# A two-layer hybrid backbone on one core: the down products of the expert passes one step further behind

## The chip, the cores and the metric

The kernel runs on one core of a Trainium2 chip. The metric is the device time in microseconds (us) of one execution, as the median of several runs; lower is better.

## The reference

The model has two layers over 512 tokens of width 1024 (256 of context, 256 latent). Each layer mixes tokens (a gated long convolution, a pooling mixer and an eight-head latent attention, joined by one output projection) and then mixes channels: a dense SwiGLU in layer 0, and in layer 1 a top-2-of-8 expert SwiGLU on the 256 latent tokens only. The change is in the experts:

```python
def swiglu(h, wg, wu, wd):
    return (jax.nn.silu(h @ wg) * (h @ wu)) @ wd

def moe_swiglu(h, w_router, wg, wu, wd):
    logits = (h @ w_router).astype(F32)
    top_val, top_idx = lax.top_k(logits, TOP_K)
    gates = jax.nn.softmax(top_val, axis=-1)
    comb = jnp.sum(jax.nn.one_hot(top_idx, N_EXPERTS, dtype=F32) * gates[..., None], axis=-2)
    out = jnp.zeros(h.shape, F32)
    for e in range(N_EXPERTS):
        out = out + comb[..., e:e + 1] * swiglu(h, wg[e], wu[e], wd[e]).astype(F32)
    return out.astype(h.dtype)
```

Here h is 256 x 1024, wg and wu are 1024 x 2816 and wd is 2816 x 1024 for each of 8 experts, all in fp32.

## The kernel before

**Passes.** The experts' part is eight passes, `expert_pass(i)` for i = 0 to 7, one for each expert. (Two further pairs of passes stand behind a branch on the number of tokens of an expert; they are not taken with these inputs.) For each expert up to 128 tokens are gathered by a matmul with a selection matrix (`gather`, for two experts at a time), and the result of pass i is spread back to the 256 token rows in pass i + 1 (`spread` on TensorE, `add_up` on VectorE, both at steps 2 and 4).

**Steps and granules.** The 2816 hidden columns are done in FC = 11 steps s of 256. A step has three granules of weights, each 128 x 2048 fp32 (1 MB): two for gate and up, `("gu", s, 0)` and `("gu", s, 1)`, each half of the 1024 input rows, and one for down, `("d", s, 0)`. NGR = 33 granules make a pass; `lay` writes them into memory in the order in which the program uses them, and `fpos` gives a granule's place in this order.

**Three products for one.** fp32 accuracy comes from pairs of rounded numbers: every operand has a high half (the number rounded to fp32r by a cast) and a low half (the rest), and `split3` (lines 446 to 450) issues high x high, high x low and low x high. A granule takes 4 of these triples, 12 matmuls of 512 columns.

**What each engine does in a step.** TensorE: `gate_up(s, 0)` and `gate_up(s, 1)` sum gate and up of the step into PSUM bank s % 2; `turn_h` (line 1003) transposes the gated rows in two 128 x 128 transposes into bank 2; `down` (line 1012) multiplies these with the down granule and sums over all steps into banks 4 and 5. ScalarE: `high(i, j)` (line 1505) makes the high half of granule j; Silu of the gate (line 1530); `high_turned` (line 1514), the high half of the transposed rows. VectorE: `low(i, j)` (line 2272) makes the low half of a granule; the product of Silu and up, `hh` (line 2298); `low_turned` (line 2281), the low half of the transposed rows. In pass 0, VectorE also runs `plan_passes`, a series of small operations on the routing tables, at the end of steps 1 to 7, and ScalarE `diagonal`, eight activations of 128 x 128, at the end of step 0. In the last pass GpSimd adds the residual (`add_residual`, lines 2471 and 2473).

**The two rings.** SP loads granules into six raw buffers: granule n goes into its buffer when VectorE has made the low half of granule n - 6 (`expert_stream`, line 2390). The high and low halves have three slots: `high(i, j)` waits until TensorE has used granule j - 3 (the counter `x_used`), `low(i, j)` waits for `high(i, j)`, and TensorE waits for `low(i, j)`.

**What sets the order.** Nothing is scheduled by a planner. Each engine's program is written out by hand in `expert_pass`, once for each engine, and each engine takes its instructions in this order; the three orders and the order of the granules in memory have to agree. TensorE's order of a step is `gu(s,0)`, transposes of step s - 1, `gu(s,1)`, `down(s-1)`; in the last step the transposes of step 10 stand in the middle of `down(9)`. At the start of a pass the place in the ring also holds the previous pass's last granules; ScalarE and VectorE there save the previous output (`save_y`, `split_y`, lines 1498 and 2230).

Of the kernel before, what the change touches and what calls it, by code (L numbers as in the profile page):

```python
# [13 lines left out]
F32 = mybir.dt.float32  # L14
# [3 lines left out]
ALU = mybir.AluOpType  # L18
ACT = mybir.ActivationFunctionType
# [26 lines left out]
RING = 3  # L46
# [21 lines left out]
def ffn_order():  # L68

    order = []  # L70
    for s in range(FC):
        order += [("gu", s, 0), ("gu", s, 1)]
        if s:
            order.append(("d", s - 1, 0))
    return order + [("d", FC - 1, 0)]


# [59 lines left out]
def build(nc, io, table):  # L137
    with ExitStack() as ctx:
# [211 lines left out]
        def x_slot(j):  # L350

            return (j + XOFF) % RING

        def tokens_of(i):

            own = slice(P * (i % 2), P * (i % 2) + P)
            if (i // 2) % 2:
                return odd_hi[:, :, own], odd_lo[:, :, own]
            own = slice(256 + P * (i % 2), 384 + P * (i % 2))
            return hT_hi[:, :, own], hT_lo[:, :, own]  # L360
# [23 lines left out]
        order = ffn_order()  # L384
        fpos = {x: i for i, x in enumerate(order)}

# [38 lines left out]
        def _(eng):  # L425
# [543 lines left out]
            def expert_pass(i):  # L969
# [41 lines left out]

                def down(s, fs=(0, 1)):
                    j = fpos[("d", s, 0)]
                    hi, lo = granule_of(j)
                    eng.wait_ge(x_tlo, FC * i + s + 1)
                    if s == 0 and i:
                        eng.wait_ge(x_y, 2 * i)
                    for f in fs:
                        a = slice(P * f, P * f + P)
                        for n in range(2):  # L1020
                            cs = slice(1024 * f + 512 * n, 1024 * f + 512 * n + 512)
                            last = split3(PS[:, 4 + n, :], f_hi[:, s % 2, a], f_lo[:, s % 2, a], hi[:, cs], lo[:, cs],
                                          s == 0 and f == 0, s == FC - 1 and f == 1)
                    if fs[-1]:
                        last.then_inc(x_used, 1)

                m = i // 2
                for s in range(FC):
                    if s == 0:
                        eng.wait_ge(x_glo, 4 * m + 2)  # L1030
                    gate_up(s, 0)
                    if s:
                        turn_h(s - 1)
                    if s == 0:
                        eng.wait_ge(x_glo, 4 * m + 4)
                    gate_up(s, 1)
                    if s == FC - 1:
                        down(s - 1, (0,))
                        turn_h(s)
                        down(s - 1, (1,))  # L1040
                    elif s:
                        down(s - 1)
                    if i and i not in LAST and s in (2, 4):
# [5 lines left out]
                    if i == 0 and s == 2:  # L1049
                        gates()  # L1050
                down(FC - 1)

# [58 lines left out]
        def _(eng):  # L1111
# [395 lines left out]
            def expert_pass(i):  # L1507
# [8 lines left out]
                if i:  # L1516
                    for j in range(0 if i in LAST else 1, RING):
                        high(i, j)
                    if i not in LAST:
                        save_y(i)  # L1520
                for s in range(FC):
                    if s:
                        high_turned(s - 1)
                    if s + 1 < FC:
                        for j in range(fpos[("gu", s + 1, 0)] if s else RING, fpos[("gu", s + 1, 1)] + 1):
                            high(i, j)
                    else:
                        high(i, fpos[("d", s, 0)])
                    eng.wait_ge(x_used, NGR * i + fpos[("gu", s, 1)] + 1)
                    act(sg[:, s % 2, :], PS[:, s % 2, 0:256], ACT.Silu).then_inc(x_silu, 1)  # L1530
                    if s + 1 < FC:
                        high(i, fpos[("d", s, 0)])
                    else:
                        high_turned(s)
                        if i + 1 not in LAST:
                            high(i + 1, 0)
# [80 lines left out]
        def _(eng):  # L1617
# [650 lines left out]

            def low(i, j, halves=(0, 1)):
                eng.wait_ge(x_hi, NGR * i + j + 1)  # L2270
                q = slice(1024 * halves[0], 1024 * halves[-1] + 1024)
                last = v.tensor_tensor(w_lo[:, x_slot(j), q], x_raw(NGR * (i % 2) + j)[:, q],  # L2272
                                       w_hi[:, x_slot(j), q].bitcast(F32), ALU.subtract)
                if halves[-1]:
                    last.then_inc(x_lo, 1)

            def expert_pass(i):
# [11 lines left out]
                for s in range(FC):  # L2289
                    if s:  # L2290
                        low_turned(s - 1)
                    if s + 1 < FC:
                        for j in range(fpos[("gu", s + 1, 0)] if s else RING, fpos[("gu", s + 1, 1)] + 1):
                            low(i, j)
                    else:
                        low(i, fpos[("d", s, 0)], (0,))
                    eng.wait_ge(x_silu, FC * i + s + 1)
                    v.tensor_tensor(hh[:, s % 2, :], PS[:, s % 2, 256:512], sg[:, s % 2, :],
                                    ALU.mult).then_inc(x_h, 1)
                    low(i, fpos[("d", s, 0)], (0, 1) if s + 1 < FC else (1,))  # L2300
                    if i and i not in LAST and s in (2, 4):
# [183 lines left out]
def lay(inputs):  # L2485
# [17 lines left out]
    def swiglu(wg, wu, wd):  # L2503
# [4 lines left out]
        d5 = wd.reshape(n, FC, 2, P, D)  # L2508
        for i, (kind, s, half) in enumerate(ffn_order()):
            if kind == "gu":  # L2510
# [108 lines left out]
```

## Time and profile before

| What | Value |
|---|---|
| Median of 3 runs | 1689.28 us |
| The runs | 1684.3, 1690.0, 1689.28 us |
| Span of the profiled execution | 1686.8 us |
| TensorE busy (matmuls) | 1611.4 us, 96% |
| TensorE weight loads busy | 1269.6 us, 75% |
| VectorE busy | 1289.9 us, 76% |
| ScalarE busy | 897.8 us, 53% |
| Mean granted TensorE clock | 0.982 |
| Bytes read from HBM | 401.03 MB, 238 GB/s over the span |

The span runs from the first to the last instruction of one profiled execution; for this execution no other time was taken, so its span stands for it, and the median of the runs is 2.5 us above the span. Shares of busy time are averages over the whole program. The expert passes take the last 800 us of it, and in them all shares are higher than in the table. Matmuls are pipelined: a matmul of 512 columns is recorded with a duration of about 0.39 us, though the next starts 0.23 us after it, so durations of matmuls overlap and the distance of their starts is the better measure. In waits, the engine named behind the arrow is the one whose signal came last.

### The profile page before, as it was taken

Reading aid. Unit: us, or ns where it says so; the run is one execution under the profiler, and the core shown is the slowest. Engines: PE = TensorE matmul, PEld = TensorE weight load, DVE = VectorE, ACT = ScalarE, POOL = GpSimd, SP = SyncE. Lnnn points to the kernel's source line nnn. Section 1 sums busy time; section 2 is a strip of 40 time slices with the busy share of each in tenths; the row PEclk is TensorE's granted clock in tenths of the full one; section 3 lists DMA queues with packets and bytes.
Section 4 is the critical chain, followed back from the end, with each engine's and each line's share of the span. In section 5 each row is a group of like instructions: output and inputs, shape, how many; then the busy total and the mean of one; then the engine's idle time right before and its main releaser. Section 6 shows DMA issues by size and latency. Waiting matters only on the chain.

```text
span 1686.8 us, 19520 instructions
## 1 busy us (share of the span) xinstructions
PE 1611.4 (96%) x7452; PEld 1269.6 (75%) x7452; DVE 1289.9 (76%) x1723; ACT 897.8 (53%) x1029; POOL 40.7 (2%) x40
## 2 busy tenths in 40 slices
PE   5999999899999999999899999999999999999996
PEld 2785567778888888786587778888888888888875
DVE  3944473698777865765768998898988889898997
ACT  3324363332222222444657777767777776777764
POOL 1000000000000000000000000000000000000050
PEclk8999999899999999999989999999999999999999
DMA  9225511363455544232147999899989999899982
GB/s 392 86 75 196 222 54 45 131 228 130 170 193 207 203 171 150 74 122 94 43 175 302 361 361 337 348 359 353 359 349 357 346 359 352 342 350 374 366 318 114
DMA packets 55972, 403.43 MB, mean 239 GB/s; under 512 B 6417, under 2 KB 6449, under 8 KB 8769
## 3 DMA queue, kind: packets, MB, share of 16 engines
q1 hardware_dynamic: 53712, 387.47, 60.3%
q0 software_dynamic: 2160, 14.63, 2.3%
q8 instruction: 62, 1.02, 0.2%
q14 instruction: 38, 0.30, 0.1%
HBM read 401.03 MB, written 1.05 MB: 238 GB/s over the span
## 4 chain that ended last, share of the span: by engine, by line
PE 74%; DVE 16%; ACT 5%; issue 3%; DMA 2%; SPq 0%; DVEq 0%; ACTq 0%
PE PS L448 20%; PE PS L450 20%; PE PS L449 20%; DVE w_lo L2272 6%; PE PS L753 2%; DVE w_lo L1633 2%; DMA arena<-in_ada 2%; ACT w_hi L1505 1%; DVE arena L1646 1%; PE PS L1008 1%; DVE XT L1999 1%; PE PS L765 1%; PE PS L778 1%; PE PS L732 1%; PE PS L458 1%
## 5 line engine op out<-in xcount | busy, mean ns | idle before, releaser
L2272 DVE TENSOR_TENSOR w_lo<-arena,w_hi 128x2048 fp32r<-128x2048 f32 (+1 forms) x136 | 305.9, 2254 | 43.3 <-ACT w_hi L1505 43.3
L2272 DVE TENSOR_TENSOR w_lo<-raw,w_hi 128x2048 fp32r<-128x2048 f32 (+1 forms) x133 | 298.9, 2251 | 32.9 <-ACT w_hi L1505 32.4
L1505 ACT CAST w_hi<-arena 128x2048 fp32r<-128x2048 f32 x132 | 251.5, 1909 | 46.2 <-PE PS L450 46.2
L1505 ACT CAST w_hi<-raw 128x2048 fp32r<-128x2048 f32 x129 | 246.9, 1916 | 43.5 <-PE PS L450 43.5
L448 PE MATMUL PS<-hT_hi,w_hi 128*128 128x512 f32 (+1 forms) x576 | 216.1, 375 | 8.6 <-DVE hT_lo L1779 6.9
L449 PE MATMUL PS<-hT_lo,w_hi 128*128 128x512 f32 (+1 forms) x576 | 213.7, 371 | 0.0
L450 PE MATMUL PS<-hT_hi,w_lo 128*128 128x512 f32 (+1 forms) x576 | 213.5, 371 | 0.0
L448 PE MATMUL PS<-w_hi,hT_hi 128*128 128x512 f32 (+1 forms) x448 | 178.5, 398 | 0.9 <-DVE w_lo L1633 0.6
L450 PE MATMUL PS<-w_hi,hT_lo 128*128 128x512 f32 (+1 forms) x448 | 174.6, 390 | 0.0
L449 PE MATMUL PS<-w_lo,hT_hi 128*128 128x512 f32 (+1 forms) x448 | 173.5, 387 | 0.0
L448 PE MATMUL PS<-w_hi,f_hi 128*128 128x512 f32 x352 | 140.4, 399 | 2.1 <-DVE f_lo L2281 2.1
L1633 DVE TENSOR_TENSOR w_lo<-raw,w_hi 128x2048 fp32r<-128x2048 f32 (+1 forms) x54 | 122.3, 2265 | 24.1 <-ACT w_hi L1127 23.9
L449 PE MATMUL PS<-w_lo,f_hi 128*128 128x512 f32 x352 | 139.0, 395 | 0.0
L450 PE MATMUL PS<-w_hi,f_lo 128*128 128x512 f32 x352 | 138.7, 394 | 0.0
L448 PE MATMUL PS<-w_hi,odd_hi 128*128 128x512 f32 x336 | 135.5, 403 | 0.0
L1127 ACT CAST w_hi<-raw 128x2048 fp32r<-128x2048 f32 (+1 forms) x54 | 102.2, 1892 | 60.8 <-PE PS L450 52.1
L448 PEld LDWEIGHTS PS<-hT_hi,w_hi 128*128 128x128 f32 x576 | 109.4, 190 | 30.1 <-DVE hT_lo L1779 7.6
L450 PE MATMUL PS<-w_hi,odd_lo 128*128 128x512 f32 x336 | 131.8, 392 | 0.0
L449 PE MATMUL PS<-w_lo,odd_hi 128*128 128x512 f32 x336 | 131.0, 390 | 0.0
L450 PEld LDWEIGHTS PS<-hT_hi,w_lo 128*128 128x128 f32 x576 | 109.5, 190 | 18.7
L449 PEld LDWEIGHTS PS<-hT_lo,w_hi 128*128 128x128 f32 x576 | 109.6, 190 | 18.3
L1999 DVE SCALAR_TENSOR_TENSOR XT<-PS,mod,XT 128x256 f32<-128x256 f32 x200 | 84.7, 476 | 33.6 <-PE PS L450 33.2
(322 smaller groups left out, 2536.0 us busy)
## 6 DMA issues: line engine op xcount, KB each, us to landing
raw<-in_moe SPq DMA_DIRECT2D x132, 1024.0 KB, 5.2
arena<-in_moe SPq DMA_DIRECT2D x132, 1024.0 KB, 5.2
raw<-in_ffn SPq DMA_DIRECT2D x33, 1024.0 KB, 4.8
raw<-in_dot SPq DMA_DIRECT2D x28, 1024.0 KB, 4.8
raw<-in_ada SPq DMA_DIRECT2D x17, 1024.0 KB, 6.5
raw<-in_out SPq DMA_DIRECT2D x8, 1024.0 KB, 4.9
raw<-in_inb SPq DMA_DIRECT2D x8, 960.0 KB, 4.7
raw<-in_ina SPq DMA_DIRECT2D x5, 1024.0 KB, 5.2
```

Of the source, the lines that this page charges most:

```text
L448: mm(out, s_hi, m_hi, start=start, stop=False)
L449: mm(out, s_hi, m_lo, start=False, stop=False)
L450: return mm(out, s_lo, m_hi, start=False, stop=stop)
L458: i = mm(o[32 * k:32 * k + 32, :], cpad[:, 4 * half + k, :], w[:, 512 * k:512 * k + 512], start=half == 0, stop=half == 1)
L732: i = mm(o[:, 256 * j:256 * j + 256], wuq[:, k, h, :], cqT[:, k, 256 * s:256 * s + 256], start=k == 0, stop=k == KQ - 1)
L753: i = mm(o[:, q], qT[0:96, n // 2, a:a + P], KT[0:96, h, 0:512 if s else 256], start=True, stop=True)
L765: i = nc.tensor.transpose(o[:, to:to + P], prob[:, u % 4, at:at + P], ident[:, :])
L1127: nc.scalar.copy(w_hi[:, slot[n], 0:w], raw_at(n)[:, 0:w]).then_inc(act_done, 1)
L1505: nc.scalar.copy(w_hi[:, x_slot(j), :], x_raw(n)).then_inc(x_hi, 1)
L1633: v.tensor_tensor(w_lo[:, slot[n], 0:w], raw_at(n)[:, 0:w], w_hi[:, slot[n], 0:w].bitcast(F32), ALU.subtract).then_inc(dve_done, 1)
L1999: v.scalar_tensor_tensor(out=XT[:, k, q], in0=o[:, q], scalar=mod[:, l, j + k, s:s + 1], in1=XT[:, k, q], op0=ALU.mult, op1=ALU.add).then_ ...
L2272: last = v.tensor_tensor(w_lo[:, x_slot(j), q], x_raw(NGR * (i % 2) + j)[:, q], w_hi[:, x_slot(j), q].bitcast(F32), ALU.subtract)
```

## The change

The granules of an expert pass are used, and stored in memory, in another order: in step s TensorE does both gate-up halves of step s, then the transposes of the gated rows of step s - 1, then the down product of step s - 2. The first two steps of a pass have no down product, and three stand after the eleventh step's gate-up halves, with the last transposes between the first and the second of them. The new function `pass_order` gives this order, and `next_granules` gives for each step the granule that ScalarE and VectorE prepare before the Silu and the gated rows of the step (`ahead`) and those that they prepare after the turned rows of the step before (`behind`). The turned rows of step s - 1 are now split after the Silu and the gated product of step s, not ahead of them. The cut of a low half into two pieces in the last step goes. The dense feed forward of layer 0 keeps its order (`ffn_order`). No instruction of TensorE, ScalarE or GpSimd is added or removed; VectorE has one instruction fewer in each pass.

```diff
@@ -73,6 +73,16 @@
         if s:
             order.append(("d", s - 1, 0))
     return order + [("d", FC - 1, 0)]
+
+
+def pass_order():
+
+    order = []
+    for s in range(FC):
+        order += [("gu", s, 0), ("gu", s, 1)]
+        if s > 1:
+            order.append(("d", s - 2, 0))
+    return order + [("d", FC - 2, 0), ("d", FC - 1, 0)]
 
 
 def filter_beside(b):
@@ -351,6 +361,14 @@
 
             return (j + XOFF) % RING
 
+        def next_granules(s):
+
+            if s == 0:
+                return [RING], []
+            if s == FC - 1:
+                return [fpos[("d", s - 1, 0)]], [fpos[("d", s, 0)]]
+            return [fpos[("gu", s + 1, 0)]], [fpos[("gu", s + 1, 1)], fpos[("d", s - 1, 0)]]
+
         def tokens_of(i):
 
             own = slice(P * (i % 2), P * (i % 2) + P)
@@ -382,7 +400,7 @@
             return raw[:, place[g], :] if place[g] < RING else first_raw[place[g] - RING]
 
         order = ffn_order()
-        fpos = {x: i for i, x in enumerate(order)}
+        fpos = {x: i for i, x in enumerate(pass_order())}
 
         def width(kind):
             return 4 * HB if kind == "inb" else GRAN
@@ -1009,37 +1027,32 @@
                                                    ident[:, :])
                     last.then_inc(x_turned, 1)
 
-                def down(s, fs=(0, 1)):
+                def down(s):
                     j = fpos[("d", s, 0)]
                     hi, lo = granule_of(j)
                     eng.wait_ge(x_tlo, FC * i + s + 1)
                     if s == 0 and i:
                         eng.wait_ge(x_y, 2 * i)
-                    for f in fs:
+                    for f in range(2):
                         a = slice(P * f, P * f + P)
                         for n in range(2):
                             cs = slice(1024 * f + 512 * n, 1024 * f + 512 * n + 512)
                             last = split3(PS[:, 4 + n, :], f_hi[:, s % 2, a], f_lo[:, s % 2, a], hi[:, cs], lo[:, cs],
                                           s == 0 and f == 0, s == FC - 1 and f == 1)
-                    if fs[-1]:
-                        last.then_inc(x_used, 1)
+                    last.then_inc(x_used, 1)
 
                 m = i // 2
                 for s in range(FC):
                     if s == 0:
                         eng.wait_ge(x_glo, 4 * m + 2)
                     gate_up(s, 0)
-                    if s:
-                        turn_h(s - 1)
                     if s == 0:
                         eng.wait_ge(x_glo, 4 * m + 4)
                     gate_up(s, 1)
-                    if s == FC - 1:
-                        down(s - 1, (0,))
-                        turn_h(s)
-                        down(s - 1, (1,))
-                    elif s:
-                        down(s - 1)
+                    if s:
+                        turn_h(s - 1)
+                    if s > 1:
+                        down(s - 2)
                     if i and i not in LAST and s in (2, 4):
                         spread(i, s // 4)
                     if i % 2 and i + 1 < NE and s in (3, 5, 7, 9):
@@ -1048,6 +1061,8 @@
                         turn_pick(m)
                     if i == 0 and s == 2:
                         gates()
+                turn_h(FC - 1)
+                down(FC - 2)
                 down(FC - 1)
 
             def last_spread(i):
@@ -1519,18 +1534,16 @@
                     if i not in LAST:
                         save_y(i)
                 for s in range(FC):
+                    ahead, behind = next_granules(s)
+                    for j in ahead:
+                        high(i, j)
+                    eng.wait_ge(x_used, NGR * i + fpos[("gu", s, 1)] + 1)
+                    act(sg[:, s % 2, :], PS[:, s % 2, 0:256], ACT.Silu).then_inc(x_silu, 1)
                     if s:
                         high_turned(s - 1)
-                    if s + 1 < FC:
-                        for j in range(fpos[("gu", s + 1, 0)] if s else RING, fpos[("gu", s + 1, 1)] + 1):
-                            high(i, j)
-                    else:
-                        high(i, fpos[("d", s, 0)])
-                    eng.wait_ge(x_used, NGR * i + fpos[("gu", s, 1)] + 1)
-                    act(sg[:, s % 2, :], PS[:, s % 2, 0:256], ACT.Silu).then_inc(x_silu, 1)
-                    if s + 1 < FC:
-                        high(i, fpos[("d", s, 0)])
-                    else:
+                    for j in behind:
+                        high(i, j)
+                    if s == FC - 1:
                         high_turned(s)
                         if i + 1 not in LAST:
                             high(i + 1, 0)
@@ -2266,13 +2279,10 @@
                                                   op0=ALU.mult, op1=ALU.add)
                 last.then_inc(x_late, 1)
 
-            def low(i, j, halves=(0, 1)):
+            def low(i, j):
                 eng.wait_ge(x_hi, NGR * i + j + 1)
-                q = slice(1024 * halves[0], 1024 * halves[-1] + 1024)
-                last = v.tensor_tensor(w_lo[:, x_slot(j), q], x_raw(NGR * (i % 2) + j)[:, q],
-                                       w_hi[:, x_slot(j), q].bitcast(F32), ALU.subtract)
-                if halves[-1]:
-                    last.then_inc(x_lo, 1)
+                v.tensor_tensor(w_lo[:, x_slot(j), :], x_raw(NGR * (i % 2) + j), w_hi[:, x_slot(j), :].bitcast(F32),
+                                ALU.subtract).then_inc(x_lo, 1)
 
             def expert_pass(i):
 
@@ -2287,17 +2297,16 @@
                     if i not in LAST:
                         split_y(i)
                 for s in range(FC):
-                    if s:
-                        low_turned(s - 1)
-                    if s + 1 < FC:
-                        for j in range(fpos[("gu", s + 1, 0)] if s else RING, fpos[("gu", s + 1, 1)] + 1):
-                            low(i, j)
-                    else:
-                        low(i, fpos[("d", s, 0)], (0,))
+                    ahead, behind = next_granules(s)
+                    for j in ahead:
+                        low(i, j)
                     eng.wait_ge(x_silu, FC * i + s + 1)
                     v.tensor_tensor(hh[:, s % 2, :], PS[:, s % 2, 256:512], sg[:, s % 2, :],
                                     ALU.mult).then_inc(x_h, 1)
-                    low(i, fpos[("d", s, 0)], (0, 1) if s + 1 < FC else (1,))
+                    if s:
+                        low_turned(s - 1)
+                    for j in behind:
+                        low(i, j)
                     if i and i not in LAST and s in (2, 4):
                         (add_up if i < NE else add_late)(i, s // 4)
                     if i % 2 and i + 1 < NE:
@@ -2506,7 +2515,7 @@
         gu = out.reshape(n, 3 * FC, P, 4, 2, 256)
         g6, u6 = (w.reshape(n, 2, 4, P, FC, 256) for w in (wg, wu))
         d5 = wd.reshape(n, FC, 2, P, D)
-        for i, (kind, s, half) in enumerate(ffn_order()):
+        for i, (kind, s, half) in enumerate(pass_order()):
             if kind == "gu":
                 gu[:, i, :, :, 0, :] = g6[:, half, :, :, s, :].transpose(0, 2, 1, 3)
                 gu[:, i, :, :, 1, :] = u6[:, half, :, :, s, :].transpose(0, 2, 1, 3)
```

How the instructions move, at the start of a pass. ScalarE first, at the start of pass 4, from the casts of the saved output on. `w_hi` is the high half of a granule, the `x_full` semaphore in its wait counts up with the raw buffers and so tells the granules apart (full3 is granule 3 of this pass, full4 is 4, full5 is 5, full0 is 6, full1 is 7); `ACTIVATE` is the Silu, `f_hi` the high half of the turned rows. Before:

```order
L1498 CAST y_hi<-PS 128x512
L1505 CAST w_hi<-arena 128x2048 [waits x_full3,x_used]
L1530 ACTIVATE arena<-PS 128x256 [waits x_used]
L1505 CAST w_hi<-arena 128x2048 [waits x_full4,x_used]
L1514 CAST f_hi<-PS 128x256 [waits x_used,x_turned]
L1505 CAST w_hi<-arena 128x2048 [waits x_full5,x_used]
L1505 CAST w_hi<-raw 128x2048 [waits x_full0,x_used]
L1530 ACTIVATE arena<-PS 128x256 [waits x_used]
L1505 CAST w_hi<-raw 128x2048 [waits x_full1,x_used]
```

And after, at the same place of ScalarE's program:

```order
L1513 CAST y_hi<-PS 128x512
L1520 CAST w_hi<-arena 128x2048 [waits x_full3,x_used]
L1541 ACTIVATE arena<-PS 128x256 [waits x_used]
L1520 CAST w_hi<-arena 128x2048 [waits x_full4,x_used]
L1541 ACTIVATE arena<-PS 128x256 [waits x_used]
L1529 CAST f_hi<-PS 128x256 [waits x_used,x_turned]
L1520 CAST w_hi<-arena 128x2048 [waits x_full5,x_used]
L1520 CAST w_hi<-raw 128x2048 [waits x_full0,x_used]
L1520 CAST w_hi<-raw 128x2048 [waits x_full1,x_used]
```

The cast of granule 5 stood behind the turned rows of step 0 and ahead of the second Silu; now it stands behind both. Granule 5 was the first half of step 2's gate-up, and is now the second half of it (granule 4, which was the first down granule, is now the first half).

TensorE at the start of pass 2, where it waits for a new granule or for a product of another engine. The rows left out are the other eleven matmuls of a granule. `w_hi,odd_hi` is the first matmul of a gate-up half, `w_hi,f_hi` that of a down product, and `ident,arena` the transposes. Before, from the second gate-up half of step 0 on:

```order
L448 MATMUL PS<-w_hi,odd_hi 128x512 [waits x_lo,x_gathered_lo]
...
L448 MATMUL PS<-w_hi,odd_hi 128x512 [waits x_h,x_lo]
...
L1008 MATMUL PS<-ident,arena 128x128 [waits x_turned_lo,x_h]
...
L448 MATMUL PS<-w_hi,odd_hi 128x512 [waits x_lo]
...
L448 MATMUL PS<-w_hi,f_hi 128x512 [waits x_y_split,x_turned_lo,x_lo]
```

And after, from the same matmul to the first down product:

```order
L466 MATMUL PS<-w_hi,odd_hi 128x512 [waits x_lo,x_gathered_lo]
...
L466 MATMUL PS<-w_hi,odd_hi 128x512 [waits x_h,x_lo]
...
L466 MATMUL PS<-w_hi,odd_hi 128x512 [waits x_lo]
...
L1026 MATMUL PS<-ident,arena 128x128 [waits x_turned_lo,x_h]
...
L466 MATMUL PS<-w_hi,odd_hi 128x512 [waits x_h,x_lo]
...
L466 MATMUL PS<-w_hi,odd_hi 128x512 [waits x_lo]
...
L1026 MATMUL PS<-ident,arena 128x128 [waits x_turned_lo,x_h]
...
L466 MATMUL PS<-w_hi,f_hi 128x512 [waits x_y_split,x_turned_lo,x_lo]
```

The transposes of step 0 stand behind the second half of step 1, and the first down product stands behind six gate-up halves where it stood behind four.

## Rows read from the trace of the kernel before

**Rows 1.** Busy time by stretch (us busy, count), one pass; last: clock, DMA share, GB/s
```profile
990.00:1086.00 96.00, 95.88 (x442) 77.98 (x441) 85.62 (x68) 68.91 (x60) 0.00 (x0) 1.00 0.90 345
```

**Rows 2.** Waits, 900 to 1650 us: who on whom, us total, times, longest
```profile
ACT f_hi L1514 <- PE PS L1008: 112.0, 83, 2.9
...
PEld PS L1008 <- DVE arena L2298: 7.0, 10, 1.1
```

**Rows 3.** Timeline of TensorE, one step: start, us, what
```profile
1109.09 0.38 PE L1008 MATMUL PS<-ident,arena 128*128 128x128 f32 x2
...
1109.23 0.48 PE L448 MATMUL PS<-w_hi,odd_hi 128*128 128x512 f32 x1
...
1109.54 0.39 PE L449 MATMUL PS<-w_lo,odd_hi 128*128 128x512 f32 x1
...
1112.07 0.39 PE L448 MATMUL PS<-w_hi,f_hi 128*128 128x512 f32 x1
...
1114.86 0.39 PE L448 MATMUL PS<-w_hi,odd_hi 128*128 128x512 f32 x1
...
1117.58 0.38 PE L1008 MATMUL PS<-ident,arena 128*128 128x128 f32 x2
```

**Rows 4.** Timeline of ScalarE, the same step (bracket: idle before, releaser)
```profile
1109.51 0.37 ACT L1514 CAST f_hi<-PS 128x256 fp32r<-128x256 f32 x1 [1.96 <-PE PS L1008]
1109.78 1.91 ACT L1505 CAST w_hi<-arena 128x2048 fp32r<-128x2048 f32 x1
...
1115.06 1.92 ACT L1505 CAST w_hi<-raw 128x2048 fp32r<-128x2048 f32 x1 [0.60 <-PE PS L450]
```

**Rows 5.** Timeline of VectorE, the same step
```profile
1111.72 2.29 DVE L2272 TENSOR_TENSOR w_lo<-arena,w_hi 128x2048 fp32r<-128x2048 f32 x1 [0.20 <-ACT w_hi L1505]
```

**Rows 6.** Timeline of VectorE at the start of pass 2, and one row of ScalarE
```profile
1080.60 6.70 DVE L2272 TENSOR_TENSOR w_lo<-raw,w_hi 128x2048 fp32r<-128x2048 f32 x3 [1.37 <-ACT w_hi L1505]
...
1082.59 1.92 ACT L1505 CAST w_hi<-raw 128x2048 fp32r<-128x2048 f32 x1 [0.22 <-PE PS L450]
...
1087.21 1.28 DVE L2230 TENSOR_TENSOR y_lo<-PS,y_hi 128x512 fp32r<-128x512 f32 x2
1088.41 2.28 DVE L2272 TENSOR_TENSOR w_lo<-arena,w_hi 128x2048 fp32r<-128x2048 f32 x1
1090.61 0.41 DVE L2298 TENSOR_TENSOR arena<-PS,arena 128x256 f32<-128x256 f32 x1
```

**Rows 7.** Timeline of TensorE, the same place
```profile
1090.55 0.39 PE L450 MATMUL PS<-w_hi,odd_lo 128*128 128x512 f32 x1
1091.08 0.44 PE L1008 MATMUL PS<-ident,arena 128*128 128x128 f32 x2
```

**Rows 8.** Timeline of pass 0: three waits of TensorE, one row of VectorE
```profile
897.67 0.50 PE L448 MATMUL PS<-w_hi,hT_hi 128*128 128x512 f32 x1 [0.29 <-DVE w_lo L2272]
...
904.52 0.47 PE L448 MATMUL PS<-w_hi,f_hi 128*128 128x512 f32 x1 [0.81 <-DVE f_lo L2281]
...
923.30 0.42 DVE L2281 TENSOR_TENSOR f_lo<-PS,f_hi 128x256 fp32r<-128x256 f32 x1
...
923.87 0.47 PE L448 MATMUL PS<-w_hi,f_hi 128*128 128x512 f32 x1 [0.30 <-DVE f_lo L2281]
```

**Rows 9.** Timeline of TensorE, last pass, while GpSimd works
```profile
1625.65 0.44 PE L1008 MATMUL PS<-ident,arena 128*128 128x128 f32 x2 [0.62 <-DVE arena L2298]
```

**Rows 10.** Timeline of TensorE after its longest idle stretches; a window by stretch
```profile
41.74 0.77 PE L448 MATMUL PS<-hT_hi,w_hi 128*128 128x512 f32 x1 [3.29 <-DVE hT_lo L1779]
...
45.20 0.39 PE L450 MATMUL PS<-hT_hi,w_lo 128*128 128x512 f32 x1
...
40.00:45.00 5.00, 3.26 (x8) 2.61 (x9) 5.00 (x14) 3.07 (x8) 0.00 (x0) 0.50 0.98 402
...
1673.41 0.50 PE L965 MATMUL PS<-y_hi,pickT 128*128 128x512 f32 x1 [2.00 <-DVE y_lo L2230]
```

**Rows 11.** DMA issues of expert weights, 990 to 1600 us
```profile
DMA to landing us min/median/max: 4.6/5.3/7.9
```

## The prediction

> **What bounds the kernel now.** I read the table of busy time by stretch first. The expert passes are eight stretches of 96 to 100 us, from about 887 us to 1671 us of the span; [rows 1] gives one window of 96 us in them: TensorE is busy 95.88 us of it at a granted clock of 1.00, VectorE 85.62, ScalarE 68.91. The reader is to see that TensorE is full, and that VectorE has only some 10 us left in 96. Busy time alone could mislead, since matmuls overlap, so the next view is the table of waits over the passes [rows 2]: ScalarE stood 112 us before the cast of the turned rows, which no one missed, and TensorE's weight loads stood 7.0 us before the transposes, for the gated rows of VectorE. That is nearly all that TensorE waits for here. The timeline of one step [rows 3] gives the prices. The pair of transposes starts at 1109.09, the next pair at 1117.58: a step of 8.49 us, for 36 matmuls and one pair. Twelve matmuls and the pair take 1112.07 - 1109.09 = 2.98, the twelve of the down product 1114.86 - 1112.07 = 2.79. Nothing stands idle between them. So in the middle of a pass the time is the number of matmuls, and the change leaves this number as it is; it can act only through TensorE's few waits and through waits that it makes.
>
> **The supply of granules.** Each granule of weights passes three slots. ScalarE casts it (high half) as soon as the granule three places earlier has been used, VectorE then makes the low half, and only then may TensorE start it. From [rows 4] and [rows 5]: the product that frees a slot ends in the row where the next one starts, 1114.86, and the cast starts at 1115.06, 0.20 later. A small cast or Silu (128x256) holds ScalarE 0.27 (1109.51 to 1109.78). The cast starts at 1109.78 and its low half at 1111.72, 1.94 later, and takes 2.29. A waiting matmul starts 0.15 after VectorE's end (923.30 + 0.42 = 923.72, matmul at 923.87) [rows 8], and the one behind it another 0.08 late (0.31 apart in place of 0.23). I count in these.
>
> **Part 1: the middle of a pass (s = 2 to 9).** I call the four pieces G0(s) and G1(s) (gate-up halves), T (transposes) and D (down). Before: G0(s) T(s-1) G1(s) D(s-1). After: G0(s) G1(s) T(s-1) D(s-2). The cast of G1(s+1) now stands behind Silu(s) and the cast of the turned rows, both of which need the end of G1(s). Counted from that end: Silu at 0.20, turned rows at 0.47 (the transposes' result is there at 0.42, 1109.09 to 1109.51), cast of G1(s+1) at 0.74, low half from 2.68 to 4.97. TensorE meanwhile does T, D and G0, 2.98 + 2.79 = 5.77. Margin 0.65 after the 0.15. The other two granules have over 1 us. T(s-1) and D(s-2) now use what was ready a step ago. Cost 0, and the cover is that 0.65; VectorE's work in a step stays 3 x 2.29 + 2 x 0.4, 7.7 of 8.49.
>
> **Part 2: the start of each pass, the term that decides.** At s = 1 there is no D yet (D(0) comes at s = 2), so six gate-up halves follow each other: G0(0) G1(0) G0(1) G1(1) T(0) G0(2) G1(2) T(1) D(0). ScalarE's order is written by the same rule as in the middle: cast of G0(2), Silu(1), turned rows (0), cast of G1(2), cast of D(0). The slot of G1(2) was freed by G0(1), long before; but its cast is behind Silu(1), which waits for the end of G1(1). From there the supply chain needs 0.20 + 0.27 + 0.27 + 1.94 + 2.29 + 0.15 = 5.12, and TensorE has only T(0) and G0(2) to do, 2.98. It stands 2.14, and with the 0.08 behind it loses 2.2. In before, the corresponding wait does not exist, since D(0) was the fifth granule. ScalarE takes its instructions in the order of the program: in [rows 2] it stood 112 us for transposes while the cast behind had its slot free. The wait comes in all eight passes: 8 x 2.2 = 17.6 us. In pass 0 the eight small activations of `diagonal` stand ahead of the cast of G0(2), so part of the wait may fall one piece earlier, at G0(2); the later cast, of G1(2), still has to follow Silu(1), which starts when G1(1) ends, so I keep the same sum. Behind the stall everything has time: D(0)'s low half ends 7.2 after the end of G1(1), needed at 8.1; the SP queue and the transfers see their slots freed later by the stall alone, and at worst 7.9 us to landing [rows 11] stand against the two steps between casts of one buffer, 16.98, less the 1.94 and 2.29 until it is released: 12.7. Bounds for this term: 0 if something covers it, 8 x 2.7 = 21.6 if VectorE's low half should start only after other work of 0.5.
>
> **Part 3: waits that go.** (a) At the start of passes 1 to 7 VectorE is a chain: three low halves in 6.70, two of the saved output in 1.28, one more low half, and then the gated rows at 1090.61 [rows 6], for which T(0) waits: it starts 0.53 after the matmul before it in place of 0.23 [rows 7]. T(0) now stands behind G1(1). What is late next is that G1(1) itself: its low half was done at 1090.69, TensorE would start it at 1090.78. The chain starts earlier after the change, since the cast of the next pass's first granule no longer waits for the late T(10): the cast that waits longest, for the end of D, starts at 1082.59 [rows 6]; from there 1.94, one low half 2.2, the output's 1.28 and the last low half 2.2 end at about 1090.2. So all 0.3 is kept: 7 x 0.3 = 2.1. (b) In pass 0 VectorE also plans the later passes, in many small operations, ahead of the low half of the turned rows, and D waits (the first of the five waits is for a granule): idle 0.29, 0.81 and three times about 0.30, of which the first stands in [rows 8]; each costs its idle time, plus 0.39 - 0.23 = 0.16 and 0.08. Sum 2.0 + 5 x 0.24 = 3.2. After the change that low half stands ahead of the planning, with a step to spare. The planning now uses up the margin of the granules: VectorE has 8.49 - 7.7 = 0.8 free in a step and the planning wants more than that, so the margin shrinks in each step. I take 3.0, bounds 0.5 and 3.2. (c) In the last pass GpSimd's residual slows VectorE's low halves, and TensorE waits for VectorE in three steps, 0.62 in the one shown [rows 9]. VectorE's work is the same after, it is the bound there, and the loss stays: 0, bounds -1 and +1.
>
> **Sum.** 17.6 - 2.1 - 3.0 = +12.5 us on the profiled execution's 1686.8 us of span: 1699.3. The runs shown have a median of 1689.3 (1684.3 to 1690.0), 2.5 above that span, which I carry along: 1701.8.
>
> **Rivals.**
> B, not slower: TensorE catches up. For it: TensorE's weight loads are busy 78 of 96 us [rows 1]; with 18 us of room a pass, a late start of 2.2 us would be made good, and only part 3 would be left: 1689.3 - 5.1 = 1684.2. It decides as soon as the matmuls behind a wait can run closer than 0.23 apart. Against: in [rows 3] they stand 0.23 apart with no wait, in any step. The Trainium skill (Perfetto Trace Analysis, Identifying the Most-Contended Engine) says to judge TensorE's headroom by its weight loads and not by matmul busy time; by it B would be likelier than I hold it, but the spacing of the starts is the stronger evidence here.
> C, the margin of 0.65 in the middle isn't there: if the low half of G1 comes 0.25 late in each of eight steps of eight passes, 16 us are added: 1718. For it: VectorE is the fullest after TensorE, 85.62 of 96 [rows 1]. Against: every count above closes with idle time left.
> D, the clock: after an idle stretch TensorE comes back at half clock. In [rows 10] it stood 3.29 us, the window around shows a granted clock of 0.50 (1.2 GHz), and the eight matmuls from 41.74 to 45.20 took 3.46 against 8 x 0.23 = 1.84: 1.6 us a time, 8 x 1.6 = 12.8: 1714.6. Against: before the last spread it stood 2.00 us, about what I expect of the new wait, and the matmul behind is 0.50, not 0.77. The Trainium skill (TensorE: Matmul & The Clock Gate, Part 1: The HAM clock gate) holds that idleness throttles the engine to half rate; that the trace agrees where it stood 3.29 and does not where it stood 2.00 is why D gets little.
>
> **How the numbers follow.** Forecast 0.76, B 0.12, C 0.07, D 0.05. The forecast's own range is 1697 to 1707: parts 2 and 3 at 2.0 to 2.5 a pass and with pass 0's saving lost at the upper end, and about 2 for the spread of the median. B and C are left out, so the range over all is 1692 to 1716. A change of 0.5%, 8.4 us, is about what a measurement can tell here from none. Slower by more: nearly all of the forecast, C and D, less a little because +12.5 is not far above 8.4: 0.80. Same: most of B and the low end of the forecast, 0.15. Faster: 0.05; all the waits that could go, 5.1 us and the last pass's, don't sum to much over 8.4.
>
> **What would show it.** In the trace after: in each pass one matmul of a gate-up half, about 6 us before the first down product begins, that waits for the low half of w with 1.7 to 2.3 us of idle time, eight times in all; seen from VectorE, an idle stretch before that low half for ScalarE's cast, and from ScalarE a wait for the matmuls ahead of Silu(1). Each pass some 1.9 longer (2.2 less 0.3). No wait for the gated rows at the transposes before the last pass, and none for the turned rows at D in pass 0. Steps of 8.49 as before in the middle. Wrong would be: no such wait (then B or a cover that I don't see), or the same wait repeated in each step (C), or matmuls 0.43 apart behind it (D).

## Result and profile after

The changed kernel takes 1705.31 us (median of 4 runs, 1700.0 to 1707.28), the kernel before 1686.79 (4 runs beside them, 1683.91 to 1690.0). The ratio is 1.0094, with a 95% interval of 1.0077 to 1.0111: slower by about 16 us. The two medians are 18.5 apart, the spans of the two profiled executions 16.7, and the 0.0094 of the ratio are 15.9; what follows explains the 16.7 of the spans. The prediction was 1701.8 us, +12.5. The profiled execution took 1705.29 us, its span is 1703.5 us (before 1686.8), and the mean granted clock fell from 0.982 to 0.974.

The window by stretch that answers to [rows 1]; the columns are the same:

```profile
990.00:1086.00 96.00, 94.10 (x430) 77.10 (x429) 83.55 (x64) 66.14 (x56) 0.00 (x0) 0.98 0.90 334
```

TensorE, full before, misses 1.9 us here, and the granted clock is not 1.00 any more. The waits over the passes, 900 to 1665 us, that answer to [rows 2] (total, times, longest):

```profile
ACT w_hi L1520 <- PE PS L468: 117.8, 139, 2.6
ACT arena L1541 <- PE PS L468: 103.0, 84, 3.4
DVE w_lo L2284 <- ACT w_hi L1520: 74.5, 183, 1.3
PEld PS L466 <- DVE w_lo L2284: 20.2, 14, 2.3
PE PS L466 <- DVE w_lo L2284: 14.5, 11, 1.9
...
ACT f_hi L1529 <- PE PS L1026: 5.4, 7, 0.8
```

The weight loads' 7.0 us for the gated rows are gone from the answer, and of ScalarE's 112 us before the cast of the turned rows 5.4 are left; it now stands before the Silu instead (L1541). New is TensorE's wait for low halves of granules: 14.5 us in 11 pieces. Seven of these are the same wait, in passes 1 to 7. At the start of pass 2, the timeline of TensorE:

```profile
1095.34 0.38 PE L1026 MATMUL PS<-ident,arena 128*128 128x128 f32 x2
...
1098.08 0.39 PE L468 MATMUL PS<-w_hi,odd_lo 128*128 128x512 f32 x1
1100.37 0.50 PE L466 MATMUL PS<-w_hi,odd_hi 128*128 128x512 f32 x1 [1.90 <-DVE w_lo L2284]
1100.70 0.52 PE L467 MATMUL PS<-w_lo,odd_hi 128*128 128x512 f32 x1
1101.02 0.63 PE L468 MATMUL PS<-w_hi,odd_lo 128*128 128x512 f32 x1
1101.44 0.63 PE L466 MATMUL PS<-w_hi,odd_hi 128*128 128x512 f32 x1
1101.87 0.63 PE L467 MATMUL PS<-w_lo,odd_hi 128*128 128x512 f32 x1
```

and of ScalarE and VectorE at the same place:

```profile
1095.53 0.38 ACT L1541 ACTIVATE arena<-PS 128x256 f32<-128x256 f32 x1 [3.27 <-PE PS L468]
1095.81 0.37 ACT L1529 CAST f_hi<-PS 128x256 fp32r<-128x256 f32 x1
1096.07 1.92 ACT L1520 CAST w_hi<-arena 128x2048 fp32r<-128x2048 f32 x1
...
1098.02 2.29 DVE L2284 TENSOR_TENSOR w_lo<-arena,w_hi 128x2048 fp32r<-128x2048 f32 x1 [1.31 <-ACT w_hi L1520]
```

The first matmul of the second gate-up half of step 2 waits: 2.29 between starts where 0.23 is the rule. ScalarE had stood 3.27 us before the Silu, with the cast behind it. From the transposes (the end of G1(1)) to the matmul it is 1100.37 - 1095.34 = 5.03; the prediction had counted 5.12. So far this is part 2. But two rows on, at 1101.02, the matmuls are 0.43 apart and last 0.63: half clock. It starts 0.65 us after the wait has ended and lasts seven matmuls. The windows say so directly; the first is around this wait, the second around the same wait in pass 4:

```profile
1096.00:1104.00 8.00, 6.10 (x20) 4.50 (x19) 6.69 (x5) 5.58 (x4) 0.00 (x0) 0.80 0.68 256
1299.00:1307.00 8.00, 6.10 (x28) 4.69 (x27) 7.16 (x5) 6.16 (x6) 0.00 (x0) 1.00 0.70 270
```

Both have 6.10 us of busy TensorE in 8; the first at a mean clock of 0.80 with 20 matmuls, the second at 1.00 with 28. Six of the seven waits (passes 1, 2, 3, 5, 6, 7) are followed by such a stretch, six or seven matmuls 0.43 apart; the one in pass 4 is not.

Where the time went, from the first matmul of each pass to that of the next (for pass 7 to the start of its last down matmul):

| Pass | Before | After | Difference |
|---|---|---|---|
| 0 | 99.36 | 97.54 | -1.82 |
| 1 | 99.98 | 102.67 | +2.69 |
| 2 | 96.44 | 99.16 | +2.72 |
| 3 | 99.93 | 102.67 | +2.74 |
| 4 (clock stays up) | 96.44 | 97.60 | +1.16 |
| 5 | 99.97 | 102.70 | +2.73 |
| 6 | 96.45 | 99.20 | +2.75 |
| 7 | 99.39 | 101.16 | +1.77 |
| sum | 787.96 | 802.70 | +14.74 |

Of the span's 16.7 us, 1.2 lie ahead of pass 0 and 0.7 behind the last down product, where the program is the same. Pass 4 against the others separates the two costs: the clock takes 2.73 - 1.16 = 1.57 us a time. The rest, +1.16, is the wait (2.29 - 0.23 + 0.08 = 2.14) less 0.30 for the transposes that no longer wait (0.24 behind the matmul before them at 1095.34; 0.53 in [rows 7]) and less about 0.7 that the prediction did not have. Most of that 0.7 is in the steps. The transposes of two neighbouring steps, which answer to the first and last row of [rows 3]:

```profile
1132.06 0.38 PE L1026 MATMUL PS<-ident,arena 128*128 128x128 f32 x2
1132.19 0.47 PE L466 MATMUL PS<-w_hi,f_hi 128*128 128x512 f32 x1
...
1135.06 0.39 PE L466 MATMUL PS<-w_hi,odd_hi 128*128 128x512 f32 x1
...
1140.50 0.38 PE L1026 MATMUL PS<-ident,arena 128*128 128x128 f32 x2
```

A step is 8.44 where it was 8.49, some 0.5 over a pass. The rows show where in the step: before, the gate-up half behind the transposes took 2.84 (1109.23 to 1112.07 in [rows 3]) and the other one 2.72 (1114.86 to 1117.58); now both stand clear of the transposes and take 5.44 together (1135.06 to 1140.50), 0.12 less. The down product, which now stands behind the transposes, takes 2.87 (1132.19 to 1135.06) where it took 2.79 (1112.07 to 1114.86), 0.08 more. Why the gate-up half loses more behind the transposes than the down product does is not shown, nor where the last 0.2 of the 0.7 is.

In pass 0 the turned rows are no longer waited for (the two later waits that [rows 8] shows, and two more like them); the new wait stands there too, in two pieces. This is the first, for granule 4:

```profile
896.77 0.50 PE L466 MATMUL PS<-w_hi,hT_hi 128*128 128x512 f32 x1 [1.24 <-DVE w_lo L2284]
```

and the second, for granule 5, has 0.37 us of idle time. All five waits of before are gone here, 3.2 us by the prediction's count; the two new ones cost 2.1 and the shorter steps give 0.7, which makes the table's -1.8. The clock stays up behind the 1.24 us. In the last pass, during GpSimd's residual, three waits of 0.24 to 0.29 us for granules take the place of those that [rows 9] shows one of:

```profile
1648.35 0.50 PE L466 MATMUL PS<-w_hi,odd_hi 128*128 128x512 f32 x1 [0.29 <-DVE w_lo L2284]
```

### The profile page after: what moved, and what is told of

It is laid out like the page before. It is cut to its first block, busy times and chain, and to the rows that moved or that the text cites. A ratio compares the mean times of both kernels' runs of the same rounds, so it can differ in the third digit from the quotient of the medians.

```text
span 1703.5 us, 19504 instructions
## 1 busy us (share of the span) xinstructions
PE 1617.1 (95%) x7452; PEld 1280.1 (75%) x7452; DVE 1289.3 (76%) x1715; ACT 896.1 (53%) x1029; POOL 42.8 (3%) x40
## 4 chain that ended last, share of the span: by engine, by line
PE 80%; DVE 11%; ACT 4%; issue 3%; DMA 2%; SPq 0%; DVEq 0%; ACTq 0%
PE PS L466 22%; PE PS L468 21%; PE PS L467 21%; DVE w_lo L2284 2%; PE PS L771 2%; DVE w_lo L1646 2%; DMA arena<-in_ada 2%; DVE arena L1659 1%; PE PS L796 1%; PE PS L783 1%; DVE XT L2012 1%; PE PS L750 1%; ACT w_hi L1520 1%; PE PS L1026 1%; PE PS L476 1%
## 5 line engine op out<-in xcount | busy, mean ns | idle before, releaser
L2284 DVE TENSOR_TENSOR w_lo<-arena,w_hi 128x2048 fp32r<-128x2048 f32 x132 | 305.6, 2317 | 46.5 <-ACT w_hi L1520 45.8
L2284 DVE TENSOR_TENSOR w_lo<-raw,w_hi 128x2048 fp32r<-128x2048 f32 x129 | 297.9, 2312 | 34.8 <-ACT w_hi L1520 34.2
L466 PE MATMUL PS<-w_hi,f_hi 128*128 128x512 f32 x352 | 146.0, 415 | 0.1
L1646 DVE TENSOR_TENSOR w_lo<-raw,w_hi 128x2048 fp32r<-128x2048 f32 (+1 forms) x54 | 122.4, 2266 | 23.9 <-ACT w_hi L1142 23.7
```

The lines of the kernel that those rows point to most:

```text
L466: mm(out, s_hi, m_hi, start=start, stop=False)
L1646: v.tensor_tensor(w_lo[:, slot[n], 0:w], raw_at(n)[:, 0:w], w_hi[:, slot[n], 0:w].bitcast(F32), ALU.subtract).then_inc(dve_done, 1)
L2284: v.tensor_tensor(w_lo[:, x_slot(j), :], x_raw(NGR * (i % 2) + j), w_hi[:, x_slot(j), :].bitcast(F32), ALU.subtract).then_inc(x_lo, 1)
```

## Experiments

**Theory.** The letters here are those of the expectations, not of the prediction's rivals. (A) The waits of passes 1 to 7 come from the place of one cast in ScalarE's program, and the half clock comes from these waits. **Rivals:** (B) six gate-up halves in a row drain the three slots whatever ScalarE's order is; (C) the half clock has another cause than the wait.

**1. The cast of granule 5 ahead of the second Silu.**

```diff
         def next_granules(s):
...
+            if s == 1:
+                return [fpos[("gu", 2, 0)], fpos[("gu", 2, 1)]], [fpos[("d", 0, 0)]]
             if s == FC - 1:
```

> The changed kernel with one thing different: in step 1 the cast and the low half of granule 5 (the second gate-up half of step 2) stand ahead of the second Silu. Theory A (the new wait of 1.90 us at the start of passes 1 to 7 comes from this cast standing behind Silu(1), and TensorE's half clock behind it comes from the wait): the wait and the stretches of matmuls 0.43 us apart both go. From the changed kernel's 1705.3 that takes 7 x 2.14 = 15.0 for the waits, 6 x 1.57 = 9.4 for the clock and about 1.9 in pass 0: about 1679, 0.5% under the kernel before. Rival B (the wait comes from the granule supply as such, six gate-up halves in a row drain the ring, whatever the order of ScalarE): the wait moves to another granule and most stays, about 1700. Rival C (the half clock is independent of the wait): the waits go and the clock stays, about 1688.

Measured: 1680.3 us (5 runs, 1678.41 to 1683.19), ratio to before 0.9949, interval 0.9935 to 0.9962. No matmul waits in passes 1 to 6, none is slow. Its window for [rows 1], and the place of the wait:

```profile
990.00:1086.00 96.00, 96.00 (x447) 79.16 (x446) 86.69 (x68) 69.95 (x60) 0.00 (x0) 1.00 0.94 352
```

```profile
1088.87 0.38 PE L1028 MATMUL PS<-ident,arena 128*128 128x128 f32 x2
...
1091.63 0.39 PE L470 MATMUL PS<-w_hi,odd_lo 128*128 128x512 f32 x1
1091.85 0.39 PE L468 MATMUL PS<-w_hi,odd_hi 128*128 128x512 f32 x1
```

The same two matmuls are 0.22 apart. B and C fall; about 25 us hang on the place of one cast and its low half. The passes 1 to 6 are 98.9 and 95.4 us, 1.07 shorter than before: 0.30 for the transposes and 0.77 as in the section above. This version beats both kernels.

It also answers a question by its end. All kernels have the 2.00 us wait ahead of the last spread ([rows 10], last row). Here it reads:

```profile
1661.69 0.65 PE L985 MATMUL PS<-y_hi,pickT 128*128 128x512 f32 x1 [2.00 <-DVE y_lo L2245]
1662.13 0.63 PE L986 MATMUL PS<-y_lo,pickT 128*128 128x512 f32 x1
1662.56 0.63 PE L985 MATMUL PS<-y_hi,pickT 128*128 128x512 f32 x1
```

The same wait, and half clock behind it, which the kernel before did not show. The length of a wait alone does not decide. The other kernels bear this out: behind this wait the eight matmuls run at full clock in the kernel before, in the changed kernel and in experiments 4 and 6, and in experiments 2, 3 and 5 the last two or three of them are 0.38 to 0.43 us apart.

**2 and 3. The wait filled, wholly and by half.** The granule is as late as in the changed kernel, but TensorE does matmuls that nobody reads meanwhile (8, or 4 with `range(4)`).

```diff
                 def gate_up(s, half):
                     j = fpos[("gu", s, half)]
+                    if s == 2 and half == 1 and 0 < i < NE:
...
+                        for _ in range(8):
+                            mm(PS[:, 7, :], pickT[:, (i - 1) % 2, 0:P], y_hi[:, 0:512], start=True, stop=True)
                     if j:
                         hi, lo = granule_of(j)
```

> The changed kernel with eight extra matmuls of 512 columns (their result is overwritten and read by nobody) ahead of the wait for granule 5 in passes 1 to 7; eight take 1.84 us of the 1.90 us of idle time, so that TensorE waits no longer than before by the clock on the wall but does not stand idle. Theory A (idleness costs the clock): no matmuls 0.43 apart at the pass starts, the 9.4 us of the clock go, the 15 us of the waits stay: about 1696. Rival C (the clock falls for another reason, for example the run of six gate-up halves without a down product): no change, 1705.

> As the kernel with eight, but with four extra matmuls: 0.92 us filled, about 1.0 us of idle time left. If the clock falls by the length of the idle time, fewer of the seven passes show half clock than the six of the changed kernel: I expect 0 to 2, 1696 to 1699. If any idle time does it, six again and 1705. Rival C: 1705.

Measured: 1694.96 us with eight (6 runs; ratio 1.0036, 1.0024 to 1.0048) and 1695.13 with four (6 runs; 1.0038, 1.0025 to 1.0052). With four, at the same place of pass 2:

```profile
1091.83 1.09 PE L1003 MATMUL PS<-y_hi,pickT 128*128 128x512 f32 x4
1093.87 0.50 PE L466 MATMUL PS<-w_hi,odd_hi 128*128 128x512 f32 x1 [0.95 <-DVE w_lo L2291]
1094.21 0.40 PE L467 MATMUL PS<-w_lo,odd_hi 128*128 128x512 f32 x1
```

No stretch at half clock behind the wait in any pass of either; passes 1 to 6 take 101.1 and 97.6 us, as pass 4 of the changed kernel does. So idleness costs the clock, 10 us in all, and half of the idle time filled is enough here: the seven waits that are left with four matmuls have 0.95 or 0.96 us of idle time. More matmuls made the kernel 10 us faster. It stays slower than before: the waits remain.

**4. The kernel before, planning behind the turned rows.** Part 3b by itself.

```diff
                     if s:
                         low_turned(s - 1)
+                        if i == 0:
+                            plan_passes(s - 1)
...
-                    if i == 0:
-                        plan_passes(s)
```

> The kernel before with one thing different: in pass 0 VectorE's planning operations of a step stand behind the low half of the turned rows instead of ahead of it. My part 3b says that the four waits of TensorE for the turned rows in pass 0 (idle 0.81 and three times 0.30) are the planning's fault and worth 2.7 us: pass 0 takes 99.36 - 2.7 = 96.7 us, the kernel 1684.1. Rival: the planning then delays the granules' low halves by as much, TensorE waits for these, and pass 0 stays at 99.4, 1686.8.

Measured: 1685.86 us (10 runs), ratio 0.9979 (0.997 to 0.9988), where 1684.1 was expected; the kernel before took 1688.71 beside it (19 runs), so the gain is 2.9. Pass 0 takes 96.67 us, 2.69 less, to the expected 96.7; of its five waits one is left, 0.29 for granule 5.

**5. The chain shorter by one small cast?**

```diff
+                    if s == 1:
+                        high(i, behind[0])
                     if s:
                         high_turned(s - 1)
-                    for j in behind:
+                    for j in behind[1 if s == 1 else 0:]:
                         high(i, j)
```

> The changed kernel with one thing different: in step 1 the cast of granule 5 stands behind Silu(1) still, but ahead of the cast of the turned rows. That is 0.27 us of ScalarE less in the chain: 1.63 us of idle time in place of 1.90 in passes 1 to 7. For the waits alone: 7 x 0.27 = 1.9 less. If the clock falls by the same cause as in the changed kernel with about the same chance a pass: 1703.4. If 0.27 us less already spares some of the stretches at half clock (four extra matmuls, 1.0 us of idle time, spared all): each spared is worth 1.57 us, down to 1694 with all.

Measured: 1705.36 us (4 runs; 1.01, 1.0083 to 1.0117). The wait did not get shorter; it is 2.23 us:

```profile
1100.13 0.50 PE L466 MATMUL PS<-w_hi,odd_hi 128*128 128x512 f32 x1 [2.23 <-DVE w_lo L2286]
```

```profile
1095.25 1.90 ACT L1520 CAST w_hi<-arena 128x2048 fp32r<-128x2048 f32 x1
1097.04 0.37 ACT L1529 CAST f_hi<-PS 128x256 fp32r<-128x256 f32 x1
...
1097.45 0.42 DVE L2293 TENSOR_TENSOR f_lo<-PS,f_hi 128x256 fp32r<-128x256 f32 x1 [1.64 <-ACT f_hi L1529]
1097.79 2.28 DVE L2286 TENSOR_TENSOR w_lo<-arena,w_hi 128x2048 fp32r<-128x2048 f32 x1
```

From the matmul before to this one it is 2.61, 0.32 more than in the changed kernel. My expectation forgot VectorE's order. There the low half of the turned rows stands ahead of granule 5's, and it now waits for a cast that stands behind the large one. The two programs have to be moved together. Five of the seven passes had slow stretches, two (2 and 5) had none.

**6. The wait longer.** Three copies of 512 columns on ScalarE ahead of the cast of granule 5.

```diff
+                    if s == 1 and 0 < i < NE:
+                        for o in (rows[:, :], A(10752, 512), A(19776, 512)):
+                            nc.scalar.copy(o, fing[:, 0:512])
                     for j in behind:
```

> The changed kernel with three extra copies of 512 columns on ScalarE (into regions that nobody reads) between the turned rows and the cast of granule 5, in passes 1 to 7. I estimate 0.5 us each, from 0.58 for a cast of 512 columns out of PSUM: 1.5 us more in the chain, idle time 3.4 us. Theory A: 7 x 1.5 = 10.5 for the waits, half clock in all seven passes (1.6 more): 1717, and more if a longer wait also keeps the clock down longer. Rival (the wait is not set by this chain): unchanged, 1705.

Measured: 1718.29 us (4 runs; 1.0175, 1.0158 to 1.0192). Pass 2 again:

```profile
1105.43 0.79 PE L466 MATMUL PS<-w_hi,odd_hi 128*128 128x512 f32 x1 [3.46 <-DVE w_lo L2287]
1106.02 0.63 PE L467 MATMUL PS<-w_lo,odd_hi 128*128 128x512 f32 x1
```

The idle time is 3.46, 1.56 more, and times seven that is 10.9; all seven passes have slow stretches. In passes 1, 2, 4 and 6 the clock is already down when the wait ends; in passes 3, 5 and 7 it falls 1.5 us later. In pass 1 twelve matmuls are 0.43 apart, about twice as many as in the others. The copies held ScalarE for 1.56 us (1099.58 to 1101.14), and the wait grew by the same: the chain through ScalarE sets it.

Together: of seven waits each, none was followed by half clock at 0.95 us of idle time, six at 1.90, five at 2.23, seven at 3.46. The record has one more length: the first wait of pass 0, 1.20 to 1.25 us in the changed kernel and in experiments 1, 2, 3, 5 and 6, was followed by full clock all six times. Six and five of seven are too few cases to tell 1.90 from 2.23.

## Why the prediction came out as it did

The direction was right and the sum 12.5 against a measured +16 (ratio 1.0094). That the sum came this near is luck, as the end of this section shows. Point by point:

- **What bounds (the middle of a pass).** Right: no wait there in passes 1 to 6, and the margin of G1 sufficed. Cost 0 was a little off: the steps are 0.05 us shorter, which with a smaller remainder makes 0.7 to 0.8 a pass. The 0.05 comes from what stands behind the transposes: a gate-up half there took 0.12 more than one elsewhere, the down product takes 0.08 more. [Rows 3] had the 2.84 and the 2.72 already; the prediction took the time of a step for the number of its matmuls.
- **Part 2, the new wait.** Right in place, cause and size: idle 1.90, lost 2.14, expected 2.14 and 2.2. Experiment 1 shows the cause. It occurs seven times, not eight. In pass 0 it comes in two pieces, 1.24 and 0.37 of idle time, together 2.1 lost.
- **Part 3a.** Right: 0.30 in each of seven passes.
- **Part 3b.** The mechanism was right: experiment 4 returned 2.69 of the five waits' 3.2, since one of them was for a granule and not for the turned rows. In pass 0 the prediction's terms give 2.2 - 3.0 = -0.8, the trace -1.82: the granule's wait went too, and the shorter steps, which had no term, give 0.7.
- **Part 3c.** Costed at nothing, bounds -1 to +1. The last pass comes out about 1.0 better than its neighbours (+1.77 against +2.73), the lower bound. In experiment 1 it is the same, 99.39 to 97.40, against 1.07 in the other passes.
- **Rival D is the step that failed.** It was held to be another world than the forecast, at 0.05, and it came on top of it: 6 x 1.57 = 9.4 us. The size of one, 1.6 from [rows 10], was right, the number not: six, not eight. The reason for the low chance was wrong: I took the 2.00 us wait before the last spread, after which the kernel before ran at full clock, as proof that such a wait is harmless. The clock may fall after the wait (0.65 us after it in the rows above), only eight matmuls followed there, and in experiment 1 the very same wait did cost the clock. One instance showed that it can go well, not that it does.

The sum again with what was measured: waits 7 x 2.14 = 15.0, clock 9.4, transposes -2.1, shorter steps about -0.7 x 7 = -4.9, pass 0 -1.8, last pass -1.0. That is +14.6, against +14.74 in the table; the last three terms are read off that table, so that it closes is no proof of them. The forecast's +12.5 came near because what it lacked, +9.4 for the clock and about -7 for the rest, have different signs; without the clock the measured terms give +5.2.

The prediction's rival B had TensorE catch up; it does not. Its rival C, waits in each step of the middle, did not occur.

## What to carry to other kernels

When a software pipeline is made deeper, write down the first steps by themselves: the order that feeds the middle on time can be late at the start, where a stage is still missing, and one cast ahead of an activation was worth 25 us here. Count a new wait of about 2 us in an otherwise full TensorE twice, once for its length and once for the clock behind it; those of 0.95 and 1.24 us cost only their length here. When two engines prepare the same operand one after the other, move it in both programs or in none.

## What the runs showed of the hardware

- The granted clock falls to half (1.2 GHz, matmuls of 512 columns 0.43 us apart in place of 0.23) after waits of about 2 us in an otherwise full TensorE, though not each time: six of seven at 1.90 us of idle time, five of seven at 2.23, none of seven at 0.95, none of six at 1.20 to 1.25 (pass 0), seven of seven at 3.46. The fall can come after the wait has ended: 0.65 us later in pass 2, 1.6 us later in pass 5 of the changed kernel. The Trainium skill (TensorE: Matmul & The Clock Gate, Part 1: The HAM clock gate) holds that the hardware looks at windows that run freely of the program. That the same 2.00 us wait before the last spread went with full clock in the kernel before and with half clock in experiment 1 fits this, and so does the different delay in passes 2 and 5; no run here tests it.
- One such fall costs 1.57 us in the changed kernel, from passes that differ in nothing else. In experiment 6 passes 2 and 4 pay about 1.3 (100.50 and 100.49 against 97.60 plus 1.56 of longer wait), and pass 1 about 2.7 (105.36 against the 101.1 of experiment 2 plus 1.56).
- Matmuls without use in the wait are faster than none: eight or four a pass brought 1705.3 down to 1695.
- The four runs of the changed kernel spread over 7 us, and the fastest, 1700.0, had the highest mean clock, 0.980 against 0.973 to 0.975. How many of the waits cost the clock differs from run to run, as far as this shows it; only one execution was profiled.
